# Row maxima and sums of an attention step: spread over the partitions by DMA through DRAM, and merged in the next step

## The chip, the core and the metric

The kernel runs on one core of a Trainium2 chip. The time is the device time of one execution in microseconds (us). The kernel before takes 1843.38 us as the median of three runs (1842.33 to 1845.44).

The engines are PE (TensorE, matrix products), DVE (VectorE), ACT (ScalarE), POOL (GpSimd) and SP (SyncE, which here only issues DMAs). Each works through its own queue of instructions in order. An instruction can wait for semaphores that other engines or DMAs raise; everything behind it on its engine waits too.

## What is computed

A decoder block of 1024 tokens and 1024 channels in float32: an input projection, a state-space branch and an attention branch, their gated sum, then a gated feed-forward network. The change is in the attention branch. There are 3 patterns (dilations 1, 4 and 16) of 8 heads each, with 64 channels a head. The part that matters:

```
s = q @ k.T + bias                       # 128 queries x 256 keys, masked
m = max(s);  p = exp(s - m);  den = sum(p)
o = (p @ v) / den;  lse = m + log(den)   # for each pattern
w = softmax(lse over the 3 patterns)
o_attn = sum(w * o)                      # merged over the patterns
```

The merge needs, for each query, the maximum m and the sum den of each pattern. The kernel keeps a running minimum of -m (`run_n`), a running sum (`run_z`) and a running numerator (`num`) and rescales them as each pattern comes in.

## The kernel before

Products are split in two parts (`whi`, `wlo` for weights, `hhi`, `hlo` for the activations), so that each block of weights takes three products for each piece: hi*hi, hi*lo and lo*hi (L909 to L911). DVE makes `whi` from the loaded `raw` (`hi`, L1673), POOL makes `wlo` (`lo`, L624), and SP loads the next `raw` when `lo` of the block two before is done (L414).

The first 700 us hold 12 attention steps, numbered a = 0 to 11: for each of 4 pairs of heads (hp), the patterns ag = 0, 1, 2. `stage_a` calls `slot` once for each step. A slot runs two things side by side: the projections of q, k and v for the next step n (three blocks b, b+1, b+2), and the attention of step a. It is cut in 12 passes, j = 0 to 11. In each pass PE first computes a quarter of a block (12 products of 512 columns), then what attention needs. Between pattern 1 and 2 there is a block of the state-space branch (`ublock`). The last slot (a = 11) has no next step; it computes instead the last such block and the first block of a gate, and POOL builds there the tables `tb`, `gg` and `gp` of the next stage.

The chain of attention in a slot is this. At even j up to 6, PE computes the scores of two blocks of queries (L1043); DVE adds the mask and takes the row maxima (L1830) and negates them into `negm` (L1834); ACT takes the exponential and its row sums into `den` (L1451); two passes later PE transposes it (L1070), ACT copies it (L1443), and PE multiplies by v (L1057). For the next step, DVE scales each half of a projected block out of PSUM (`evict`, L1796) at odd j; ACT squares it (L1394), PE sums the squares at j = 2, 4, 6, 8 (L923), ACT makes the norm factors `rn`, and POOL multiplies them in (`qk_scale`, L737).

`negm` and `den` have one value for each row, with the queries on the partitions. The merge works with channels on the partitions and queries along the free axis, so each value is needed on 64 partitions. Before, this is done in the same slot: at j = 8 and 9, DVE copies the values into 128 columns each (`stat`, two buffers `hx` and `rtmp`, L1855), and at j = 9, 10 and 11 PE transposes the copies, 16 transposes of 128x128 in a step (L1022, L1031), into PSUM. DVE then merges each half of the queries: `merge_max` (L1755 to L1758), whose result ACT exponentiates into `ab_h` (L1459), `merge_psum` (L1771, L1772) and `merge_z` (L1778, L1780); POOL merges the numerator (`rescale` L765, `weigh` L770, `normalise` L776). The first half is merged at j = 10 and 11 of the slot itself. Of the second half `merge_max` runs at j = 11, the rest in the next slot at j = 0 and 1 (after pattern 1: in `ublock`). For pattern 0 there is nothing to merge with, and the values are only copied.

The order on every engine is that of the code: each engine has its own `slot`, written out by hand, with `if` tests on j.

## Time and profile before

| | |
|---|---|
| median of 3 runs | 1843.38 us |
| the profiled execution: its own time, its span | 1847.69 us, 1845.8 us |
| PE busy | 1795.4 us (97%) |
| DVE busy | 1019.9 us (55%) |
| POOL busy | 828.6 us (45%) |
| ACT busy | 569.2 us (31%) |

The span runs from the first to the last instruction. A busy PE is one with a product in flight: 12 products of 512 columns follow each other at about 0.23 us each, and each is shown with 0.39 us. So the length of a piece of work on PE is read from the chain of work (which has the distance to the next instruction), not from the duration of one product.

The attention slots lie between 57 and 700 us. Slot a = 2 runs from about 168 us, slot a = 3 from about 215 us, the last, a = 11, from about 644 us. The three pairs of heads before the last repeat with the same pattern.

### The profile page before, as it was taken

Reading aid. Unit: us, or ns where it says so; the run is one execution under the profiler, and the core shown is the slowest. Engines: PE = TensorE matmul, PEld = TensorE weight load, DVE = VectorE, ACT = ScalarE, POOL = GpSimd, SP = SyncE. Lnnn points to the kernel's source line nnn. Section 1 sums busy time; section 2 is a strip of 40 time slices with the busy share of each in tenths; the row PEclk is TensorE's granted clock in tenths of the full one; section 3 lists DMA queues with packets and bytes.
Section 4 is the critical chain, followed back from the end, with each engine's and each line's share of the span. In section 5 each row is a group of like instructions: output and inputs, shape, how many; then the busy total and the mean of one; then the engine's idle time right before and its main releaser. Section 6 shows DMA issues by size and latency. Waiting matters only on the chain.

```text
span 1845.8 us, 23996 instructions
## 1 busy us (share of the span) xinstructions
PE 1795.4 (97%) x8628; PEld 1427.0 (77%) x8628; DVE 1019.9 (55%) x1545; ACT 569.2 (31%) x1075; POOL 828.6 (45%) x597
## 2 busy tenths in 40 slices
PE   8999999999999988999899999999999999999997
PEld 6777777777777766788788878788888888888786
DVE  6346645564664587344411232788787787634644
ACT  6533444353344423111411221543333333000000
POOL 7536444653643375554344444265555455222221
PEclk9999999999999998999999999999999999999999
DMA  4111111211111113445411134323223222345211
GB/s 172 35 40 55 47 49 40 76 40 40 47 52 47 40 52 98 110 114 147 139 68 68 68 137 159 137 80 102 69 71 99 68 94 99 126 152 195 85 53 50
DMA packets 64186, 158.00 MB, mean 86 GB/s; under 512 B 10912, under 2 KB 27680, under 8 KB 64112
## 3 DMA queue, kind: packets, MB, share of 16 engines
q1 hardware_dynamic: 51856, 145.35, 23.8%
q10 hardware_dynamic: 11792, 10.04, 2.0%
q0 software_dynamic: 464, 1.62, 0.2%
q8 instruction: 46, 0.75, 0.2%
q14 instruction: 28, 0.23, 0.0%
HBM read 123.54 MB, written 32.26 MB: 84 GB/s over the span
## 4 chain that ended last, share of the span: by engine, by line
PE 73%; issue 12%; DVE 8%; POOL 5%; ACT 1%; DMA 1%; POOLq 0%; SPq 0%; DVEq 0%
PE bank L909 9%; PE bank L911 9%; PE bank L910 9%; PE bank L1278 7%; PE bank L1280 7%; PE bank L1279 7%; PE bank L1336 4%; PE bank L1338 4%; PE bank L1337 4%; PE bank L923 2%; PE bank L1057 2%; PE bank L1070 2%; PE bank L1043 2%; POOL wlo L624 1%; POOL t L858 1%
## 5 line engine op out<-in xcount | busy, mean ns | idle before, releaser
L909 PE MATMUL bank<-hhi,whi 128*128 128x512 f32 x1024 | 421.0, 411 | 5.1 <-DVE hlo L1717 4.6
L911 PE MATMUL bank<-hhi,wlo 128*128 128x512 f32 x1024 | 405.1, 396 | 0.0
L910 PE MATMUL bank<-hlo,whi 128*128 128x512 f32 x1024 | 404.9, 395 | 0.0
L624 POOL TENSOR_TENSOR wlo<-raw,whi 128x1024 fp32r<-128x1024 f32 (+1 forms) x84 | 196.5, 2340 | 281.4 <-DVE whi L1673 279.4
L909 PEld LDWEIGHTS bank<-hhi,whi 128*128 128x128 f32 x1024 | 193.9, 189 | 52.1 <-issue 9.0
L911 PEld LDWEIGHTS bank<-hhi,wlo 128*128 128x128 f32 x1024 | 193.5, 189 | 45.2
L910 PEld LDWEIGHTS bank<-hlo,whi 128*128 128x128 f32 x1024 | 194.2, 190 | 39.6 <-issue 1.2
L1830 DVE CUSTOM_DVE_ANT_0 sp<-bank,mask 128x128 f32<-128x128 f32 (+1 forms) x192 | 56.3, 348 | 113.6 <-PE bank L1043 111.7
L1451 ACT ACTIVATE sp<-sp,negm 128x128 f32<-128x128 f32 (+1 forms) x192 | 83.9, 439 | 107.4 <-DVE negm L1834 107.3
L1673 DVE CAST whi<-raw 128x1024 fp32r<-128x1024 f32 (+1 forms) x84 | 62.3, 741 | 95.1 <-PE bank L911 64.8
L882 POOL TENSOR_TENSOR plo<-st,phi 128x512 fp32r<-128x512 f32 x60 | 79.6, 1329 | 58.7 <-ACT phi L1585 57.4
L2131 DVE CAST fhi<-ff 128x1024 fp32r (+1 forms) x44 | 31.4, 715 | 125.5 <-PE bank L1338 125.5
L1443 ACT ACTIVATE ptr<-bank 128x256 f32<-128x256 f32 (+1 forms) x96 | 45.5, 474 | 165.1 <-PE bank L1070 165.1
L1278 PE MATMUL bank<-thi,phi 128*128 128x512 f32 x240 | 94.8, 395 | 0.0
L1279 PE MATMUL bank<-tlo,phi 128*128 128x512 f32 x240 | 94.7, 395 | 0.0
L1280 PE MATMUL bank<-thi,plo 128*128 128x512 f32 x240 | 94.6, 394 | 0.0
L737 POOL TENSOR_TENSOR kn<-kn,rn 128x512 f32<-128x512 f32 x24 | 35.8, 1493 | 97.9 <-ACT rn L1405 97.9
L882 POOL TENSOR_TENSOR qlo<-pair,qhi 128x512 fp32r<-128x512 f32 x40 | 68.5, 1733 | 13.9 <-ACT qhi L1585 13.9
L1336 PE MATMUL bank<-fhi,whi 128*128 128x512 f32 x176 | 70.2, 399 | 2.3 <-DVE osb L2191 1.4
L895 POOL TENSOR_TENSOR dlo<-raw,dhi 128x1024 fp32r<-128x1024 f32 x11 | 26.8, 2437 | 100.3 <-DVE dhi L2124 100.3
L1338 PE MATMUL bank<-fhi,wlo 128*128 128x512 f32 x176 | 69.5, 395 | 0.0
L1337 PE MATMUL bank<-flo,whi 128*128 128x512 f32 x176 | 69.4, 395 | 0.0
(304 smaller groups left out, 3946.6 us busy)
## 6 DMA issues: line engine op xcount, KB each, us to landing
raw<-in_wblocks SPq DMA_DIRECT2D x98, 512.0 KB, 3.6
pair<-in_wblocks SPq DMA_DIRECT2D x40, 512.0 KB, 4.7
ff_scr<-ffo SPq DMA_DIRECT2D x22, 512.0 KB, 5.9
ff<-ff_scr SPq DMA_DIRECT2D x22, 512.0 KB, 4.0
rt<-rt_scr SPq DMA_DIRECT2D x8, 516.0 KB, 6.8
x<-in_xT SPq DMA_DIRECT2D x8, 512.0 KB, 8.7
zb_scr<-zb SPq DMA_DIRECT2D x8, 512.0 KB, 3.2
zb<-zb_scr SPq DMA_DIRECT2D x8, 512.0 KB, 3.3
```

Of the source, the lines that this page charges most:

```text
L624: pool.tensor_tensor(wlo[par][:, 0:cols], raw[par][:, 0:cols], whi[par][:, 0:cols].bitcast(F32), ALU.subtract).then_inc(lo_done, 1)
L882: pool.tensor_tensor(piece[i][1], weights(u_par)[i], piece[i][0].bitcast(F32), ALU.subtract).then_inc(lo_p, 1)
L909: nc.tensor.matmul(ps, a, x, start=start and k == k_list[0], stop=False)
L910: nc.tensor.matmul(ps, a, y, start=False, stop=False)
L911: last = nc.tensor.matmul(ps, b, x, start=False, stop=stop and k == k_list[-1])
L1278: nc.tensor.matmul(pbank(i), a[:, r], xh, start=c == 0, stop=False)
L1279: nc.tensor.matmul(pbank(i), a[:, r], xl, start=False, stop=False)
L1280: last = nc.tensor.matmul(pbank(i), b[:, r], xh, start=False, stop=c == KC // 2 - 1)
L1336: nc.tensor.matmul(ps, dhi[par][:, r], x, start=start and c == 0, stop=False)
L1337: nc.tensor.matmul(ps, dhi[par][:, r], y, start=False, stop=False)
L1338: last = nc.tensor.matmul(ps, dlo[par][:, r], x, start=False, stop=stop and c == 1)
L1451: last = act.activation(sp[:, s_ % 4, x, s0:], sp[:, s_ % 4, x, s0:], ACT.Exp, bias=negm[:, s_, x:x + 1], accum_out=den[:, s_, x:x + 1])
```

## The change

In the steps a = 0 to 10 the row values go another way. `negm` and `den` are now halves of one tile `sd` of 32 columns. At the end of pass j = 9, PE transposes `sd` once (to 32 partitions of 128), at j = 10 ACT copies the result to `st_t`, and SP writes it to DRAM (`stat_scr`), waits for that, and reads it back four times, each time one row of 1024 values to 64 partitions: into `bmd` (maxima in `bmd[:, 0]`, sums in `bmd[:, 1]`), or for pattern 0 straight into `run_n` and `run_z`. SP does this (`spread`) between its loads of weights. The merge of a step moves as a whole into the next slot: on DVE `merge_max` at j = 1 and 2, `merge_psum` at 3 and 5, `merge_z` at 3 and 6; on ACT the exponential at 3 and 4; on POOL `rescale` and `weigh` at 4 and 6, and `normalise` at 7 and 10 after pattern 2. The product with v at j = 4 and 8 on PE now also waits until `merge_psum` has read the bank. The last step keeps the old way, but its slot now has the whole merge of step 10 in front.

```diff
+            def spread(a, hp, ag):
+                sp_.wait_ge(st_copied, a + 1)
+                sp_.wait_ge(d_read, 2 * a + 1)
+                if ag == 0 and hp:
+                    sp_.wait_ge(o_ready, 2 * hp)
...
+                sp_.dma_start(stat_scr.rearrange("i x (s q) -> (i x s) q", q=P), st_t[0:32, :]).then_inc(st_out, 16)
+                sp_.wait_ge(st_out, 16 * (a + 1))
+                for i, done in enumerate((sm_in, sz_in)):
+                    to = (run_n, run_z)[i][:, :] if ag == 0 else bmd[:, i, :]
+                    for x in range(2):
+                        sp_.dma_start(to[DH * x:DH * (x + 1)], stat_scr[i, x].unsqueeze(0).broadcast_to([DH, T])).then_inc(done, 16)
...
 # POOL, slot
-                    if a and ag == 0 and j == 0:
-                        weigh(a - 1, 2, hp - 1, 1)
-                    if a and ag == 0 and j == 5:
-                        normalise(2, hp - 1, 1)
+                    if a and ag != 1 and j in (4, 6):
+                        pg, ph, h = (ag + 2) % 3, hp - (ag == 0), j // 2 - 2
+                        rescale(pg, ph, h)
+                        weigh(a - 1, pg, ph, h)
+                    if a and ag == 0 and j in (7, 10):
+                        normalise(2, hp - 1, j == 10)
...
 # PE, slot
-                    if a is not None and j in (9, 11):
+                    if n is None and j in (9, 11):
...
+                                if a and s_ % 4 == 0:
+                                    pe.wait_ge(d_read, 2 * a + s_ // 4)
...
+                        if n is not None and j == 9:
+                            pe.wait_ge(ln_done, 4 * n + 4)
+                            nc.tensor.transpose(b_nb[0:32, 0:P], sd[:].rearrange("p i x s -> p (i x s)"), ident).then_inc(mt_done, 1)
...
 # ACT, slot
+                    if a and ag != 1 and j in (3, 4):
+                        weights_exp((ag + 2) % 3, hp - (ag == 0), j - 3)
...
+                        act.activation(st_t[0:32, :], b_nb[0:32, 0:P], ACT.Copy).then_inc(st_copied, 1)
...
 # DVE, merge_max and slot
-                nn, ps = natural(run_n[:, :], ag, h), split2(b_nb[:], ag)
+                if a == LAST:
+                    dve.wait_ge(mt_done, LAST + h + 1)
+                else:
+                    dve.wait_ge(sm_in, 32 * (a + 1))
+                nn, new = natural(run_n[:, :], ag, h), split2(b_nb[:] if a == LAST else half(bmd[:, 0, :], h), ag)
...
-                TT(t_z[:], b_t[:], ab[h][:, 1, :], ALU.mult).then_inc(d_read, 1)
+                TT(t_z[:], b_t[:] if a == LAST else half(bmd[:, 1, :], h), ab[h][:, 1, :], ALU.mult).then_inc(d_read, 1)
...
+                    if a:
+                        last_step = a - 1, (ag + 2) % 3, hp - (ag == 0)
+                        if j in (1, 2):
+                            merge_max(*last_step, j - 1)
+                        if j in (3, 5):
+                            merge_psum(*last_step, j == 5)
+                        if j in (3, 6):
+                            merge_z(*last_step, j == 6)
...
-                    if a is not None and j in (8, 9):
+                    if n is None and j in (8, 9):
```

Two places show how the order moves. The first is DVE in slot a = 3, from the end of pass 0 to the first score of pass 2. Before:

```order
L1834 TENSOR_SCALAR negm<-mx 128x4 [waits dve_c]
L1771 TENSOR_TENSOR t_num<-bank,ab_h 128x512 [waits ab_exp,dt_done,pv_done]
L1772 TENSOR_TENSOR t_z<-bank,ab_h 128x512
L1796 TENSOR_TENSOR qn<-bank,rs 128x128x4 [waits groups]
L1820 COPY vv<-bank 128x512 [waits vt_done]
L1673 CAST whi<-raw 128x1024 [waits groups,loaded0]
L1778 TENSOR_TENSOR run_z<-run_z,ab_h 128x8x64
L1780 TENSOR_TENSOR run_z<-run_z,t_z 128x8x64 [waits d_read,dve_c]
L1830 ISA sp,mx<-bank,mask 128x256 [waits dve_c,s_done,h_lo]
```

After these come the other scores of pass 2, their `negm`, and then at once the second eviction of q (L1796). Now, from the last instruction of the scores of pass 2 to the cast of pass 4 (L1886 was L1834, L1846 was L1796, L1723 was L1673):

```order
L1886 TENSOR_SCALAR sd<-mx 128x2x2 [waits dve_c]
L1802 TENSOR_TENSOR ab_h<-run_n,bmd 128x512 [waits merged,sm_in]
L1803 TENSOR_TENSOR run_n<-run_n,bmd 128x8x64 [waits dve_c]
L1806 TENSOR_SCALAR ab_h<-ab_h 128x512 [waits dve_c]
L1807 TENSOR_SCALAR ab_h<-ab_h 128x512 [waits dve_c]
L1846 TENSOR_TENSOR qn<-bank,rs 128x128x4 [waits groups]
L1821 TENSOR_TENSOR t_num<-bank,ab_h 128x512 [waits ab_exp,sz_in,pv_done]
L1822 TENSOR_TENSOR t_z<-bmd,ab_h 128x512
L1828 TENSOR_TENSOR run_z<-run_z,ab_h 128x8x64
L1830 TENSOR_TENSOR run_z<-run_z,t_z 128x8x64 [waits d_read,dve_c]
L1723 CAST whi<-raw 128x1024 [waits dve_c,groups,loaded1]
```

The same four instructions of `merge_max` for the first half stand between the cast of pass 1 and the scores of pass 2. So the second eviction has eight more instructions ahead of it in this slot, and two of `merge_z` fewer.

The second place is POOL in the last slot. Before, the second merge of the numerator (L765, L770) of step 10 stands ahead of the tables:

```order
L765 TENSOR_TENSOR num<-num,ab_h 128x2x256 [waits ab_exp]
L770 TENSOR_TENSOR num<-num,t_num 128x2x256 [waits d_read,pool_c]
L624 TENSOR_TENSOR wlo<-raw,whi 128x1024 [waits hi_done]
L711 TENSOR_TENSOR tb<-ccr,b_in 128x1024 [waits bc_in,prep_b]
L712 TENSOR_TENSOR ttmp<-cci,b_in 128x8x128 [waits pool_c]
L713 TENSOR_TENSOR tb<-tb,ttmp 128x1024 [waits pool_c]
L624 TENSOR_TENSOR wlo<-raw,whi 128x1024 [waits pool_c,hi_done]
L721 TENSOR_TENSOR gg<-g_a,c_in 128x1152
```

Now (L804 was L765, L809 was L770, L661 was L624, L748 to L750 were L711 to L713, L758 to L760 were L721 to L723):

```order
L750 TENSOR_TENSOR tb<-tb,ttmp 128x1024 [waits pool_c]
L804 TENSOR_TENSOR num<-num,ab_h 128x2x256 [waits pool_c,ab_exp]
L809 TENSOR_TENSOR num<-num,t_num 128x2x256 [waits d_read,pool_c]
L661 TENSOR_TENSOR wlo<-raw,whi 128x1024 [waits hi_done]
L758 TENSOR_TENSOR gg<-g_a,c_in 128x1152
L759 TENSOR_TENSOR ttmp<-g_b,c_in 128x1152 [waits pool_c]
L760 TENSOR_TENSOR gg<-gg,ttmp 128x1152 [waits pool_c]
L758 TENSOR_TENSOR gp<-g_c,c_in 128x1024 [waits pool_c]
L759 TENSOR_TENSOR ttmp<-g_d,c_in 128x8x128 [waits pool_c]
L760 TENSOR_TENSOR gp<-gp,ttmp 128x1024 [waits pool_c]
L804 TENSOR_TENSOR num<-num,ab_h 128x2x256 [waits pool_c,ab_exp]
L809 TENSOR_TENSOR num<-num,t_num 128x2x256 [waits d_read,pool_c]
```

The first half of the numerator is merged between `tb` and `gg`, the second after all six instructions of `gg` and `gp`.

## Rows read from the trace of the kernel before

**Rows 1.** The page: busy time, share of the span, instructions.
```profile
PE 1795.4 (97%) x8628; PEld 1427.0 (77%) x8628; DVE 1019.9 (55%) x1545; ACT 569.2 (31%) x1075; POOL 828.6 (45%) x597
```

**Rows 2.** Windows, slots 3 and 11: length; busy PE, PEld, DVE, ACT, POOL; clock; DMA, GB/s.
```profile
213.00:255.00 42.00, 40.32 (x219) 30.04 (x218) 27.29 (x60) 25.69 (x55) 23.55 (x13) 1.00 0.12 38
...
663.00:700.00 37.00, 32.44 (x175) 24.72 (x174) 31.23 (x35) 16.11 (x33) 26.96 (x13) 0.95 0.19 65
```

**Rows 3.** Chain of work, step 0: start, length on the chain, what.
```profile
98.08 0.44 PE bank L1022 x4
```

**Rows 4.** Timeline of DVE, slot 3: start, length, instruction, [idle before <- releaser].
```profile
225.09 0.67 DVE L1673 CAST whi<-raw 128x1024 fp32r<-128x1024 f32 x1
...
226.74 3.09 DVE L1780 TENSOR_TENSOR run_z<-run_z,t_z 128x512 f32<-128x512 f32 x1
...
231.65 1.05 DVE L1834 TENSOR_SCALAR negm<-mx 128x4 f32<-128x4 f32 x1
232.60 1.10 DVE L1796 TENSOR_TENSOR qn<-bank,rs 128x512 f32<-128x512 f32 x1
```

**Rows 5.** Timeline of POOL, slot 3.
```profile
225.84 3.05 POOL L624 TENSOR_TENSOR wlo<-raw,whi 128x1024 fp32r<-128x1024 f32 x1 [0.77 <-DVE whi L1673]
...
231.13 1.53 POOL L737 TENSOR_TENSOR qn<-qn,rn 128x512 f32<-128x512 f32 x1
```

**Rows 6.** Timelines of DVE and POOL at the end of slot 1.
```profile
157.96 2.41 POOL L624 TENSOR_TENSOR wlo<-raw,whi 128x1024 fp32r<-128x1024 f32 x1 [0.71 <-DVE whi L1673]
158.90 1.09 DVE L1756 TENSOR_TENSOR run_n<-run_n,bank 128x512 f32<-128x512 f32 x1
```

**Rows 7.** Timeline of DVE, end of slot 2: one half of the merge.
```profile
215.18 1.04 DVE L1755 TENSOR_TENSOR ab_h<-run_n,bank 128x512 f32<-128x512 f32 x1
...
217.69 0.43 DVE L1758 TENSOR_SCALAR ab_h<-ab_h 128x512 f32<-128x512 f32 x1
```

**Rows 8.** Timelines of PE and ACT, slot 3.
```profile
222.30 0.60 PE L1005 MATMUL bank<-cst_s,vt 128*128 128x128 f32 x4
...
234.72 1.08 ACT L1394 ACTIVATE sq<-qn 128x512 f32<-128x512 f32 x1
235.95 1.10 PE L923 MATMUL bank<-sq,cst_s 128*128 128x512 f32 x2 [1.38 <-ACT sq L1394]
```

**Rows 9.** Timelines of DVE, ACT and PE, slot 2.
```profile
176.33 1.03 DVE L1673 CAST whi<-raw 128x1024 fp32r<-128x1024 f32 x1
...
184.20 0.62 ACT L1394 ACTIVATE sq<-qn 128x512 f32<-128x512 f32 x1
185.82 1.02 PE L923 MATMUL bank<-sq,cst_s 128*128 128x512 f32 x2
```

**Rows 10.** Timelines of DVE and POOL, last slot.
```profile
653.15 0.68 DVE L1820 COPY vv<-bank 128x512 f32<-128x512 f32 x1
...
663.28 2.05 DVE L1673 CAST whi<-raw 128x1024 fp32r<-128x1024 f32 x1
...
685.95 1.03 DVE L1755 TENSOR_TENSOR ab_h<-run_n,bank 128x512 f32<-128x512 f32 x1
...
657.67 2.66 POOL L711 TENSOR_TENSOR tb<-ccr,b_in 128x1024 f32<-128x1024 f32 x1
...
679.25 2.47 POOL L723 TENSOR_TENSOR gp<-gp,ttmp 128x1024 f32<-128x1024 f32 x1
```

**Rows 11.** Chain of work, last slot: start, length on the chain, what.
```profile
664.39 0.43 PE bank L909
...
667.17 0.23 PE bank L910
...
711.23 0.70 DVE zb L1789
```

**Rows 12.** DMA issues, 57 to 700 us: count, KB each, median us to landing.
```profile
raw<-in_wblocks SPq DMA_DIRECT2D x36, 512.0 KB, 3.5
...
u_scr<-utmp SPq DMA_DIRECT2D x4, 512.0 KB, 2.6
```

More of the change, by code:

```diff
@@ L189, in bass_hybrid_block @@
             mx = sb("mx", [P, 2, 2])
-            negm = sb("negm", [P, 8, 2])
-            den = sb("den", [P, 8, 2])
+            sd = sb("sd", [P, 2, 2, 8])
+            st_t = sb("st_t", [P, P])
             utmp = sb("utmp", [P, CH, NCH])
-            rtmp = sb("rtmp", [P, 2, GB, NCH // 2])
-            hx = sb("hx", [P, T])
+            bmd = sb("bmd", [P, 2, T])
             with ExitStack() as s_prep:
@@ L285, in bass_hybrid_block @@
         dhi, dlo = (dhi0, whi[1]), (dlo0, wlo[1])
-        stat = [hx[:], rtmp[:].rearrange("p a g k -> p (a g k)")]
+        negm, den = sd[:, 0], sd[:, 1]
+        stat = [bmd[:, h, :] for h in range(2)]
+        LAST = 3 * HP - 1
         bank = [ctx.enter_context(nc.psum_tensor(f"bank{i}", [P, HT], F32)) for i in range(8)]
@@ L453, in _ @@
                                   [:, bass.ds(RSTEP * hp, RB)], rt0[NST * u:NST * (u + 1)]).then_inc(rt_out, 16)
-            for n in range(B_AEND, B_E1 + 1):
+            for n in range(B_AEND, B_AEND + 3):
                 load(n, wblocks[n], n % 2)
+            spread(LAST - 3, HP - 2, 2)
+            for n in range(B_AEND + 3, B_AEND + 6):
+                load(n, wblocks[n], n % 2)
+            spread(LAST - 2, HP - 1, 0)
+            for n in range(B_AEND + 6, B_E1 + 1):
+                load(n, wblocks[n], n % 2)
+            spread(LAST - 1, HP - 1, 1)
             sp_.wait_ge(pv_done, 8 * 11)
@@ L1023, in slot @@
                         last.then_inc(mt_done, 1)
-                    if a is not None and j in (10, 11):
+                    if n is None and j in (10, 11):
                         h = j - 10
@@ L1451, in slot @@
                                 last = act.activation(sp[:, s_ % 4, x, s0:], sp[:, s_ % 4, x, s0:], ACT.Exp,
-                                                      bias=negm[:, s_, x:x + 1], accum_out=den[:, s_, x:x + 1])
+                                                      bias=negm[:, x, s_:s_ + 1], accum_out=den[:, x, s_:s_ + 1])
                             last.then_inc(exp_done, 1)
@@ L1833, in slot @@
                         link(last)
-                        V.tensor_scalar(negm[:, j:j + 2, :], mx[:], -1.0, None, ALU.mult).then_inc(smx_done, 1)
-                    if a and (ag < 2 or n is None) and j == 0:
-                        merge_psum(a - 1, (ag + 2) % 3, hp - (ag == 0), 1)
-                    if a is not None and j == 11:
+                        V.tensor_scalar(negm[:, :, j:j + 2].rearrange("p x s -> p s x"), mx[:], -1.0, None, ALU.mult).then_inc(smx_done, 1)
+                    if n is None and j == 11:
                         merge_psum(a, ag, hp, 0)
@@ L1861, in slot @@
                         gate_in(0, 0, j - 10)
-                    if a is not None and j >= 10:
+                    if n is None and j >= 10:
                         merge_max(a, ag, hp, j - 10)
-                    if a is not None and j == 11:
+                    if n is None and j == 11:
                         merge_z(a, ag, hp, 0)
-                        if n is None:
-                            merge_psum(a, ag, hp, 1)
-                            merge_z(a, ag, hp, 1)
+                        merge_psum(a, ag, hp, 1)
+                        merge_z(a, ag, hp, 1)
                 if n is None:
```

102 lines of the change are left out of this document (57 added, 45 removed).

## The prediction

> **What bounds the kernel now.** I read the page first: PE is busy for 97% of the span [rows 1]. Work taken off PE in the attention part is worth its full length, as long as nothing makes PE wait instead. So the question is what PE waits for in the slots, and whether the change adds to it. The windows of the slots show PE busy all the time but for two kinds of place: slot 3 (and 6 and 9, which repeat it) has 40.32 us of work in 42.00, and the last slot 32.44 in 37.00 at a mean clock of 0.95 [rows 2]. The timelines say why. In slot 3, PE stands for 1.38 us before the second sum of squares, until ACT has squared the second half of q; ACT stands behind the eviction of q by DVE, which DVE only reaches at 232.60 [rows 8, 4]. In slot 2 the same instruction starts without idle time, since the square ended at 184.82, a microsecond ahead [rows 9]. In the last slot the chain runs through DVE and ends at the gate's eviction at 711.23 [rows 11]: there DVE, not PE, sets the time.
>
> A second thing decides this case: DVE and POOL get in each other's way. In slot 3 the last addition to `run_z` takes 3.09 us, while `lo` is on POOL from 225.84 to 228.89 [rows 4, 5]; it ends 0.94 us after POOL's instruction does, so it stood until then. The negation of 4 values takes 1.05 us, until the end of POOL's multiplication [rows 4, 5]. But the minimum with a source in PSUM takes its usual 1.09 us in the middle of a `lo` of normal length [rows 6]. So an instruction of DVE with all its operands in SBUF waits for the instruction that POOL has begun, and one that reads PSUM does not.
>
> The Trainium skill (SBUF — State Buffer, on the shared port pair) states the same and more: a DVE instruction with two SBUF inputs and a GpSimd instruction that reads SBUF exclude each other for a whole instruction, whoever starts first. It speaks against this change, which moves a source of three DVE instructions of each half of the merge from PSUM to SBUF. By this rule, the trace agrees (3.09 against 1.09 us). Without it the sum below would come out faster; that case is a rival.
>
> **What goes.** Per step, 16 transposes in four groups, each of them 0.44 us on the chain of work [rows 3], 1.76 us; one transpose comes, at a quarter of a group, 0.11 us, or 0.2 if it costs a change of weights. I take 1.6 us a step. There are 11 such steps: -17.6 us. It counts fully, since in passes 9 to 11 PE does not wait. The copies of `negm` and `den` and the copies for pattern 0 leave DVE too, at passes where DVE has spare time; I count them at nothing.
>
> **What the new way costs by itself.** ACT's copy, SP's store and four loads are new waits: `merge_max` in pass 1 waits for the maxima. The trace has no such transfer. Lower bound: the store as `u_scr`, 2.6 us, the loads as one load of 512 KB, 3.5 us, so 6.1 us; upper bound: five such transfers one behind the other, 2.6 + 4 x 3.5 = 16.6 us [rows 12]. Four passes lie between, 10, 11, 0 and 1, of 12 products at 0.23 us and some 1 us of attention each, together 15 us. The loads are issued without waiting for each other, so I take 8 us, hidden. Loads of weights queued behind them on SP have two blocks, some 25 us, in hand. I count 0 for this, and +1 us a merge, 7 in all, at the far end.
>
> **Slots 3, 6 and 9 (merge of pattern 2).** DVE in pass 1: the eviction can start when the products end at 222.30 [rows 8]; with the copy of v and the cast (0.97 + 0.6 + 0.6 us from start to start) `merge_max` begins at 224.5. Uncontended a half takes 2.9 us, from 215.18 to 218.12 [rows 7]. But the cast has just released POOL's `lo` of 2.4 us, and it shares operands in SBUF only: the subtraction goes first, `lo` follows, the minimum waits for it. That makes 1.1 + 2.4 + 1.1 + 0.9 = 5.4 us, to 229.9. Scores of pass 2 then take 1.5 us, the negation 1.05 as before [rows 4]: 232.5. The second half: 2.9 us, to 235.4; eviction 1.0, to 236.4; square 1.1 [rows 8], to 237.5. PE arrives at 235.95 - 1.38 = 234.6. It waits 3.0 us instead of 1.4: +1.6. Behind this the lock takes its toll once more: DVE's last pair (L1778, L1780) and the negation of pass 6 alternate with `rescale`, `weigh` and `qk_scale`, so that the fourth square is about 1 us late for PE in pass 8. I take +2.5 us a slot. The ends: without the lock, the square is ready 2.4 us sooner and PE waits 0.6 us, -0.8; with one more wait for a `lo`, +3.2.
>
> **Slots 2, 5 and 8 (merge of pattern 1).** Same sequence, shorter passes of 128 columns. The cast starts at 176.33 [rows 9]; `merge_max` begins at 176.9, ends 5.4 us later at 182.3 (2.9 us if the lock didn't bind: 179.8), scores 1.1, negation 0.6 (POOL multiplies q), second half 2.9, eviction 0.6, square 0.6 [rows 9]: 188.1. PE comes at 185.82 [rows 9]. It waits 2.3 us where it did not wait. The ends are 0 (without the lock, 185.7 is in time) and +3.2. I take +2.3.
>
> In slots 1, 4, 7 and 10 the merge is only a copy of the numerator, so nothing is late: 0.
>
> **The last slot.** Here DVE is the bound. Before, `merge_max` of step 10 was done by 647.5, beside products. Now DVE is idle until its copy of v (653.15 before [rows 10], some 1.2 us earlier now) and then has 2.9 + 2.9 + 1.3 + 2.2 = 9.3 us of merge ahead of the cast of the gate's second block, where it had 4.9. The cast, at 663.28 before [rows 10], comes 3.2 us later uncontended. But POOL has `lo` and three instructions of `tb` (2.66 us the first [rows 10]) in the same stretch; each can hold an instruction of DVE for about 2 us, together up to +6. The cast frees POOL for the tables, which ended at 681.7 [rows 10]; behind them now stand `rescale` and `weigh` of the second half (1.6 us each), and DVE's second `merge_max` of step 11 (685.95 before [rows 10]) needs them. With the cast 3.2 us late: 681.7 + 3.2 + 3.2 = 688.1, +2 us. With 9 us, and 2 more for DVE's merge among the tables: 681.7 + 11 + 3.2 = 695.9, +10. There is no row for this alternation at length; I take +9, near the upper end, since [rows 4, 10] show nearly every such meeting at its full price. What follows up to 711.23 is serial and moves with it [rows 11].
>
> **Sum.** -17.6 + 3 x 2.5 + 3 x 2.3 + 9 = +5.8 us. Against the profiled execution, 1847.7 + 5.8 = 1853.5 us. That execution lies 4.3 us over the median of the runs, so the forecast is 1843.4 + 5.8, about 1849 us. The bounds of the terms: -17.6 - 2.4 + 0 + 2 = -18.0, and -17.6 + 9.6 + 9.6 + 10 = +11.6, with transfers that come late +18.6.
>
> The clock can add to this. In the last slot, after waits, six products are 0.43 us apart instead of 0.23 [rows 11], so the engine ran at 1.2 instead of 2.4 GHz for that stretch: 1.2 us lost. The wait of 1.38 us in slot 3 was followed by no such stretch (clock 1.00 [rows 2]). Waits of 2 to 3 us are in between; if each of the six did it, +7 us.
>
> **Rivals.**
> 1. *PE keeps nearly all it is given: faster.* The lock binds little and the queue on DVE has the slack to take the merge. For it: DVE is busy for only 55% [rows 1], its idle time lies just in these passes, and 4 us of copies leave it in each step. Against it: the minimum of `merge_max` meets `lo` by construction, since the cast ahead of it starts `lo`. With slots at -0.8 and 0 and the last at +5: -15 us, 1828.
> 2. *A draw.* Terms of about half the size: slots at +1 and +1.2, last slot +7: -4 us, 1840, or a little less gain, 1843.
> 3. *The transfers come late.* If the chain store, wait, four loads takes the 16.6 us of the upper bound and SP's queue adds to it, DVE stands in pass 1 with evictions behind it. Every microsecond beyond the 15 counts in six slots. At 3 us late, on top of the forecast: +18, 1867. Against it: the queue of SP is free at that point, having nothing but loads that wait for `lo`.
> 4. *The slots lose more than they gain, worse than forecast:* the clock falls in the waits. +7 us, 1856.
>
> **Chances.** Forecast with its neighbourhood (1847 to 1854) 0.33; rival 1 0.27; rival 2 0.2; rival 4 0.14; rival 3 0.06. The likeliest alone has 1845 to 1856. The range goes from 1827 to 1859: it takes in the bounds of the terms and leaves out the far transfers. A difference of 0.2% (3.7 us) is what can be told from no change. Faster by more: rival 1 and a third of rival 2, 0.34. Within: the rest of rival 2 and the edge of the forecast, 0.18. Slower by more: 0.48.
>
> **What would show it.** The transposes: on PE one instruction of 32 columns a step and a slot shorter by 1.6 us where no merge is (slots 1, 4, 7 and 10). The lock: the minimum of the first half at over 3 us instead of 1.1, in the middle of a `lo`. The queue: PE's idle time before the second sum of squares, 3.0 us in slot 3 and 2.3 in slot 2, released by ACT's square. The last slot: the cast of the second gate block some 8 us later from the slot's start, `merge_max` of the second half behind POOL's `weigh`. The transfers: DVE not waiting for DMA in pass 1. The forecast is wrong if ACT's squares come in time, that is, if slots 2 and 3 show PE at 38 of 38 and 42 of 42 us; or if DVE's wait in pass 1 names a DMA.

## The result and the profile after

The changed kernel takes 1862.2 us (median of 4 runs, 1859.2 to 1863.6); the kernel before took 1844.4 us beside it (4 runs, 1842.3 to 1845.8). The ratio is 1.0097, with a 95% interval of 1.0084 to 1.011: 17.9 us slower. The forecast was about 1849 us, by its sum 5.8 us slower, and its range ended at 1859. The profiled execution took 1861.9 us, its span 1860.0.

The table takes each slot from the start of its first transpose of v to that of the next slot, and the last slot from there to the gate's eviction [rows 11].

| slots | before, us | after, us | change of all |
|---|---|---|---|
| 0, 1, 4, 7, 10 (nothing to weigh) | 52.4, 61.1, 61.1, 61.1, 50.0 | 50.8, 59.5, 59.5, 59.5, 48.4 | -8.0 |
| 2, 5, 8 (merge of pattern 1) | 47.2, 47.2, 47.2 | 50.1, 50.1, 50.1 | +8.8 |
| 3, 6, 9 (merge of pattern 2) | 54.1, 54.2, 54.2 | 55.5, 56.6, 55.5 | +5.1 |
| last | 64.2 | 76.9 | +12.7 |

Together that is +18.6 us. What follows the last slot took 1134.6 us in the profile before and 1130.4 after. In the experiments that stretch lay anywhere from 1128.6 to 1134.6, whatever the edit, so I take nothing from this difference.

The page's busy line (busy time, share of the span, instructions) answers to [rows 1]:

```profile
PE 1787.9 (96%) x8463; PEld 1411.8 (76%) x8463; DVE 999.4 (54%) x1485; ACT 570.1 (31%) x1086; POOL 822.0 (44%) x597
```

PE has 165 instructions and 7.5 us of work fewer, not 17.6: some of its instructions got longer. The windows of slot 2, slot 3 and the last slot (length; busy PE, PEld, DVE, ACT, POOL; granted clock; DMA, GB/s) answer to [rows 2]:

```profile
175.00:213.00 38.00, 35.45 (x182) 25.62 (x181) 24.87 (x48) 17.60 (x48) 18.51 (x11) 0.96 0.15 49
213.00:255.00 42.00, 38.68 (x203) 28.05 (x202) 29.50 (x61) 22.35 (x51) 16.54 (x9) 0.96 0.19 51
663.00:700.00 37.00, 21.98 (x113) 16.09 (x112) 36.24 (x52) 9.29 (x33) 27.37 (x13) 0.72 0.20 64
```

The clock, at 1.00 before in slot 3, is at 0.96, and in the last slot at 0.72 where it was 0.95. DVE is now busy for all but 0.8 of 37 us there. PE's timelines in slots 2 and 3 (start, length, instruction, [idle before <- releaser]) answer to [rows 8, 9]:

```profile
185.01 1.10 PE L961 MATMUL bank<-sq,cst_s 128*128 128x512 f32 x2 [2.46 <-ACT sq L1434]
186.04 1.23 PE L1080 MATMUL bank<-kn,qn 64*128 64x128 f32 x8
187.20 1.12 PE L1096 MATMUL bank<-ptr,vv 128*64 128x128 f32 x8
...
236.84 1.69 PE L961 MATMUL bank<-sq,cst_s 128*128 128x512 f32 x2 [3.32 <-ACT sq L1434]
```

The waits stand where the forecast put them, at 2.46 us (forecast 2.3) and 3.32 us (3.0). Behind the first, eight score products take 1.23 us and eight products with v 1.12. Where no such wait stands, both take about 0.7 (a row of such a run follows below): PE worked at 1.2 instead of 2.4 GHz there. Such a time at the lower clock is a slow stretch in what follows. DVE and POOL in slot 2, which answer to [rows 6, 7]:

```profile
173.66 3.08 POOL L661 TENSOR_TENSOR wlo<-raw,whi 128x1024 fp32r<-128x1024 f32 x1 [3.99 <-DVE whi L1723]
...
174.61 3.06 DVE L1803 TENSOR_TENSOR run_n<-run_n,bmd 128x512 f32<-128x512 f32 x1
...
181.58 1.10 DVE L1803 TENSOR_TENSOR run_n<-run_n,bmd 128x512 f32<-128x512 f32 x1
...
183.52 0.68 DVE L1846 TENSOR_TENSOR qn<-bank,rs 128x512 f32<-128x512 f32 x1
```

The minimum of the first half meets `lo` and takes 3.06 us; that of the second half takes 1.10. In slot 3 it is 3.08. The eviction stands behind both halves. In the last slot, DVE's first `merge_max`, PE's three long waits, DVE's copies of the row values, the `weigh` that POOL does behind the tables, and the gate's eviction answer to [rows 10, 11]:

```profile
658.00 1.31 DVE L1802 TENSOR_TENSOR ab_h<-run_n,bmd 128x512 f32<-128x512 f32 x1
659.34 2.65 DVE L1803 TENSOR_TENSOR run_n<-run_n,bmd 128x512 f32<-128x512 f32 x1
662.03 1.93 DVE L1806 TENSOR_SCALAR ab_h<-ab_h 128x512 f32<-128x512 f32 x1
663.99 2.45 DVE L1807 TENSOR_SCALAR ab_h<-ab_h 128x512 f32<-128x512 f32 x1
...
667.54 1.22 PE L1080 MATMUL bank<-kn,qn 64*128 64x128 f32 x8 [3.36 <-DVE sd L1886]
...
672.74 1.12 PE L1096 MATMUL bank<-ptr,vv 128*64 128x128 f32 x8 [3.98 <-issue]
...
687.73 9.29 DVE L1911 COPY bmd<-sd 128x512 f32<-128x512 f32 x4
...
692.48 1.11 PE L1059 MATMUL bank<-cst_s,bmd 128*128 128x128 f32 x4 [5.84 <-DVE bmd L1911]
...
698.66 1.57 POOL L809 TENSOR_TENSOR num<-num,t_num 128x512 f32<-128x512 f32 x1
...
729.57 0.69 DVE L1839 TENSOR_TENSOR zb<-bank,rs 128x512 f32<-128x512 f32 x1
```

Every one of the four instructions of `merge_max` meets one of POOL's, and it takes 8.4 us instead of 2.9. The copies of the row values start 35.1 us from the slot's start, where they started 25.0 us from it before, and the four take 9.3 us instead of 7.4. The transfers, from 57 to 700 us, answer to [rows 12] (count, KB each, median us to landing):

```profile
bmd<-stat_scr SPq DMA_DIRECT2D x28, 256.0 KB, 4.5
...
stat_scr<-st_t SPq DMA_DIRECT2D x11, 16.0 KB, 1.4
```

In no slot does DVE wait for them.

### The profile page after: what moved, and what is told of

Read it like the earlier page. It is cut to its first block, busy times and chain, and to the rows that moved or that the text cites. A ratio compares the mean times of both kernels' runs of the same rounds, so it can differ in the third digit from the quotient of the medians.

```text
span 1860.0 us, 23700 instructions
## 1 busy us (share of the span) xinstructions
PE 1787.9 (96%) x8463; PEld 1411.8 (76%) x8463; DVE 999.4 (54%) x1485; ACT 570.1 (31%) x1086; POOL 822.0 (44%) x597
## 4 chain that ended last, share of the span: by engine, by line
PE 72%; issue 12%; DVE 10%; POOL 5%; DMA 1%; ACT 1%; POOLq 0%; SPq 0%; DVEq 0%
PE bank L947 9%; PE bank L949 9%; PE bank L948 9%; PE bank L1318 7%; PE bank L1320 7%; PE bank L1319 7%; PE bank L1376 4%; PE bank L1378 4%; PE bank L1377 4%; PE bank L961 2%; PE bank L1096 2%; PE bank L1080 2%; PE bank L1107 2%; DVE run_n L1803 2%; POOL wlo L661 1%
## 5 line engine op out<-in xcount | busy, mean ns | idle before, releaser
L661 POOL TENSOR_TENSOR wlo<-raw,whi 128x1024 fp32r<-128x1024 f32 (+1 forms) x84 | 197.4, 2350 | 401.9 <-DVE whi L1723 400.4
L1498 ACT ACTIVATE sp<-sp,sd 128x128 f32<-128x128 f32 (+1 forms) x192 | 83.9, 439 | 185.4 <-DVE sd L1886 185.4
L1723 DVE CAST whi<-raw 128x1024 fp32r<-128x1024 f32 (+1 forms) x84 | 64.3, 765 | 96.5 <-PE bank L949 63.5
L1846 DVE TENSOR_TENSOR vt<-bank,rs 128x512 f32<-128x512 f32 x24 | 23.3, 969 | 141.3 <-PE bank L949 141.3
L933 POOL TENSOR_TENSOR dlo<-raw,dhi 128x1024 fp32r<-128x1024 f32 x11 | 26.8, 2436 | 99.5 <-DVE dhi L2179 99.5
L961 PE MATMUL bank<-sq,cst_s 128*128 128x512 f32 x96 | 53.2, 637 | 17.6 <-ACT sq L1434 17.3
```

What stands on the lines that cost most here:

```text
L661: pool.tensor_tensor(wlo[par][:, 0:cols], raw[par][:, 0:cols], whi[par][:, 0:cols].bitcast(F32), ALU.subtract).then_inc(lo_done, 1)
L961: nc.tensor.matmul(b_nb[:], blk_ones, sq[:, gi % 2, :], start=True, stop=True).then_inc(ss_done, 1)
L1498: last = act.activation(sp[:, s_ % 4, x, s0:], sp[:, s_ % 4, x, s0:], ACT.Exp, bias=negm[:, x, s_:s_ + 1], accum_out=den[:, x, s_:s_ + 1])
```

## The experiments

Each kernel ran five rounds beside the kernel before; the figures are differences from it, by the ratio of the runs, with the interval. Most intervals are some 2.5 us to either side. The changed kernel stands at +17.9. Unless said otherwise an edit is made to the changed kernel.

**1. The second eviction ahead of the second half.**

```
-                        if j in (1, 2):
-                            merge_max(*last_step, j - 1)
+                        if j in (1, 2 if n is None else 3):
+                            merge_max(*last_step, j > 1)
```

> The changed kernel, but in the slots with projections the second half of merge_max stands in DVE's pass 3, behind the second eviction of q, instead of ahead of it. Queue theory: ACT's second square comes 2.9 us sooner, the wait of PE before the second sum of squares (3.3 us in slot 3, 2.5 in slot 2) falls to under 0.5 us in each of the six slots, and with it the stretch at the lower clock behind it (granted clock 1.00 again in slots 2 and 3): 6 x (2.5 to 3 of wait + 1.2 to 1.5 of slow products) less what the half merge now delays behind it, -14 to -22 us, 1840 to 1848 us. Lock rival: the delay is made by POOL's lo in the first half, which stays where it is, so at most 1 us a slot comes back: 1856 or more. Route rival: the DMA chain sets the time, nothing changes: 1862. The last slot, which keeps its order, stays at 12 to 13 us over before in each case.

Measured: +7.9 us (1.0043, 1.003 to 1.0057), 10 us less than the change. Slots 2 and 3 take 48.6 and 54.5 us. PE and ACT in slot 2, and PE in slot 3:

```profile
182.03 1.04 ACT L1478 ACTIVATE ab_h<-ab_h 128x1024 f32<-128x1024 f32 x1
182.98 0.61 ACT L1434 ACTIVATE sq<-qn 128x512 f32<-128x512 f32 x1
...
183.73 1.10 PE L961 MATMUL bank<-sq,cst_s 128*128 128x512 f32 x2 [1.32 <-ACT sq L1434]
184.76 0.71 PE L1080 MATMUL bank<-kn,qn 64*128 64x128 f32 x8
...
234.13 1.84 PE L961 MATMUL bank<-sq,cst_s 128*128 128x512 f32 x2 [2.28 <-ACT sq L1434]
```

The order of the queue matters, but less than expected: only 1.1 us of the wait went in slot 2 and 1.0 in slot 3, since ACT, held up by the late negation, now comes to the square after the exponential of the weights. The slow stretch went too in slots 2, 5 and 8, where the wait is 1.32 us (clock 1.00). Where it is 2.28 us, slots 3 and 6 have one (0.96 in slot 3's window) and slot 9 has none (1.00), yet all three take 54.4 to 54.5 us: at the full clock, PE waits 1.1 us more for the fourth square. So a slow stretch can cost nothing where another chain is close.

**2. The cast behind the first half.**

```
+                        if n is not None and j == 1:      # behind merge_max
+                            hi(b + 1, (par0 + 1) % 2, need=2 * b)
```

> The changed kernel, but in pass 1 the cast of the next weights, which releases POOL's lo, stands behind the first half of merge_max instead of ahead of it. Lock theory: the minimum takes 1.1 us instead of 3.06, the second square comes about 2 us sooner, PE's wait falls from 3.3 to about 1.3 us in slot 3 and from 2.5 to about 0.5 in slot 2; the clock falls in fewer slots: 6 x 2 to 3.5, -12 to -20 us, 1842 to 1850. Its price: the cast comes 4 us later, and the weights of the next block with it, which has passes in hand. Queue theory alone (the order of the eviction decides, not the meeting with lo): POOL's lo then meets the negation or the second half, and the 2 us are paid there: -3 to +2, 1859 to 1864. Route rival: no change.

Measured: +12.5 us (1.0068, 1.0054 to 1.0082), 5.4 less than the change; between the two theories. DVE in slot 2:

```profile
174.30 1.08 DVE L1803 TENSOR_TENSOR run_n<-run_n,bmd 128x512 f32<-128x512 f32 x1
...
177.87 1.55 DVE L1886 TENSOR_SCALAR sd<-mx 128x4 f32<-128x4 f32 x1
...
180.44 2.04 DVE L1803 TENSOR_TENSOR run_n<-run_n,bmd 128x512 f32<-128x512 f32 x1
...
183.32 0.68 DVE L1846 TENSOR_TENSOR qn<-bank,rs 128x512 f32<-128x512 f32 x1
```

With `lo` out of its way the first minimum takes 1.08 us. That is the lock shown by taking away what it meets: the two instructions are the same as before. But the 2 us are mostly paid again at the negation (1.55) and the second minimum (2.04, beside POOL's multiplication of q), and the eviction comes only 0.5 us sooner, 15.6 us from the slot's start instead of 16.1. So PE's wait in slot 2 is 1.96 us instead of 2.46, and the clock still falls behind it (0.96 from 171 to 213 us):

```profile
184.81 1.69 PE L961 MATMUL bank<-sq,cst_s 128*128 128x512 f32 x2 [1.96 <-ACT sq L1434]
```

The Trainium skill (SBUF — State Buffer, section Terms, on the shared port pair) says that the loser of the pair is blocked for the whole instruction of the other, and that it does not share bandwidth. The trace agrees (3.06 us beside `lo`, 1.08 us without it).

**3. Tables of the last slot behind the merge.**

```
                     if n is None and j == 4:
                         lo(B_E1 + 1, 1)
+                    if n is None and j == 6:      # POOL, behind rescale and weigh
                         g_table(0)
                         gp_table(0)
```

> The changed kernel, but in the last slot POOL does the two gate tables (six instructions, some 15 us) behind rescale and weigh of the second half of step 10 instead of ahead of them. Theory of POOL's order: DVE's second merge_max of step 11 (704.0 in the changed kernel) no longer stands behind weigh at 698.7, and the last slot gets 4 to 8 us shorter, 1854 to 1858 us; the tables end 3 us later, which PE needs only behind the gate. Rival, the lock with the tb table: the 8.4 us of the first merge_max in that slot and the late cast at 678 are made before this point, and the tables then collide with the stat copies and the gate: gain 0 to 2 us, 1860 to 1862.

Measured: +16.0 us (1.0087, 1.0072 to 1.0102); the last slot takes 76.6 us against 76.9. The rival was right. POOL's `weigh` now comes 15.4 us sooner from the slot's start, and the second `merge_max` of step 11 only 0.2 us:

```profile
680.63 2.29 POOL L809 TENSOR_TENSOR num<-num,t_num 128x512 f32<-128x512 f32 x1
...
701.22 1.04 DVE L1803 TENSOR_TENSOR ab_h<-run_n,bank 128x512 f32<-128x512 f32 x1
```

In the changed kernel `weigh` had ended at 700.23, 3.8 us before that `merge_max` began at 704.01. So it was never what DVE waited for there.

**4. The thinned transposes alone (kernel before).**

```
-                        for s_ in range(4):
+                        for s_ in range(1 if n is not None else 4):
                             last = nc.tensor.transpose(b_nb[:, s_ * P:(s_ + 1) * P], ...
```

> The kernel before, with one part of the change alone: of the four transposes of each group of negm and den only the first is done in the slots with projections (88 + 88 of 176 transposes in 11 steps become 44 instead of 176), while the merge stays where it was; so maxima and sums are wrong in three quarters of the rows, and one Ln is an Exp. Theory (PE's time counts in full): 12 transposes of about 0.11 us a step, 11 steps: -14.5 us, 1829 us. Rival (the waits of slots 3, 6 and 9 and the clock take part of it): -8 to -10 us, 1834 to 1836. Were it under -4, the gain of the change would be off the path altogether.

This kernel leaves out transposes that the result needs, and one Ln, so its values are wrong; it serves for the time alone. Measured: -7.8 us (0.9958, 0.9944 to 0.9972). That is near the rival (-8 to -10). By slots: 1, 4 and 7 are 1.2 to 1.3 us shorter, 3, 6 and 9 0.7 to 0.8, and 2, 5 and 8 only 0.2 to 0.3. In slot 2 PE stood for POOL:

```profile
182.76 0.50 PE L909 MATMUL bank<-hhi,whi 128*128 128x512 f32 x1 [0.68 <-POOL wlo L624]
```

PE was busy for the whole of slot 2 before, and still a microsecond taken off it there bought next to nothing, as the weights were not split yet.

**5. Also the square ahead of the weights on ACT** (on top of 1).

```
...
+                    if a and ag != 1 and n is not None and j == 3:    # ACT, behind square
+                        weights_exp((ag + 2) % 3, hp - (ag == 0), 0)
```

> As the run with the second eviction ahead of the second half of merge_max (1852.4 us), and on ACT the exponential of the first half's weights (1.04 us) stands behind the square in pass 3 instead of ahead of it. There the wait before the second sum of squares had fallen from 3.3 to 2.3 us in slot 3 and from 2.5 to 1.3 us in slot 2, and ACT's row showed exponentials of the scores, then the weights (1.04 us), then the square, without idle time. Theory (the rest of the wait is ACT's queue behind a late negation): each of the six waits gets 1.04 us shorter, to 1.3 and 0.3 us, and slots 2 and 3 with it: -6 us or, with less time at the low clock, -9: 1843 to 1847. Rival (the time is lost in the passes behind, the third and fourth squares): -2 us or less, 1850 to 1853.

Measured: +7.4 us (1.004, 1.0026 to 1.0054), as without this edit: the theory fell, the rival holds. PE's rows with idle time:

```profile
182.98 1.10 PE L961 MATMUL bank<-sq,cst_s 128*128 128x512 f32 x2 [0.38 <-ACT sq L1434]
185.59 0.66 PE L1096 MATMUL bank<-ptr,vv 128*64 128x128 f32 x8 [0.87 <-issue]
...
233.35 1.10 PE L961 MATMUL bank<-sq,cst_s 128*128 128x512 f32 x2 [1.34 <-ACT sq L1434]
...
244.35 1.10 PE L961 MATMUL bank<-sq,cst_s 128*128 128x512 f32 x2 [1.19 <-ACT sq L1434]
```

The first wait did get 0.94 us shorter in both slots, and new ones took its place: 0.87 us ahead of the products with v in slot 2, 1.19 at the third square in slot 3. The clock is 1.00 in both slots now, and slot 3 takes 54.8 us, no less than with the slow stretch of run 1 (54.5).

**6. Both halves behind the eviction** (on top of 5).

```
+                        if n is not None and j == 3:
+                            merge_max(*last_step, 0)
+                            merge_max(*last_step, 1)
```

> As the run before this one, and the first half of merge_max too stands behind the second eviction, so DVE does in pass 1 to 3: copy, cast, scores, negation, eviction, and then both halves of the merge. Theory (one queue: merge ahead of the scores delays negation, exponentials, square): the second square comes as in the kernel before or sooner; PE's wait there is under 0.8 us in each slot and the clock of slots 2 and 3 is 1.00. The lock moves too, since lo now meets the negation. Slots 2 and 3 reach 46.9 and 53.4 us, their lengths in the run with thinned transposes: 1840 us, with the last slot still 12 us over. Rival: the merge of 8.6 us now stands ahead of merge_psum, which PE's product with v needs in pass 4, or delays the third eviction, and the wait appears there: 1845 to 1852.

Measured: +20.7 us (1.0112, 1.0096 to 1.0127), slower than the change. Neither theory gave that size. The place is the rival's. DVE and PE in slot 2:

```profile
186.73 0.68 DVE L1823 TENSOR_TENSOR t_num<-bank,ab_h 128x512 f32<-128x512 f32 x1
187.33 0.68 DVE L1824 TENSOR_TENSOR t_z<-bmd,ab_h 128x512 f32<-128x512 f32 x1
...
188.11 0.66 PE L1096 MATMUL bank<-ptr,vv 128*64 128x128 f32 x8 [3.77 <-issue]
```

The numerator of the step before still lies in the PSUM bank into which pass 4 writes the first products with v. So the merge has only the first passes of the slot: early, it holds up the eviction; late, it holds up PE. This is the bind of the change, and my forecast did not have it, although the change itself names the new wait.

**7. Step 10 merged the old way.** The 16 transposes and the copies of step 10 are back, its merge stands in its own passes 10 and 11, and the last slot is that of before.

```
+        OLD = (LAST - 1, LAST)
...
-                    if n is None and j in (9, 11):
+                    if a in OLD and j in (9, 11):
```

> The changed kernel, but step 10 too is merged the old way (16 transposes in its own slot, the merge in its passes 10 and 11 and in passes 0 and 1 of the last slot), so that the last slot is that of the kernel before. Theory (the last slot as such costs 12.7 us, by the merge that moved into it): that comes back less 1.6 us of transposes in slot 10: -11 us, 1851. Rival (the last slot is late for reasons that remain, such as the stat copies that meet POOL's tables): -3 to -5 us, 1857 to 1859.

Measured: +6.5 us (1.0035, 1.0023 to 1.0047), 11.4 less than the change, as expected. The gate's eviction, 76.9 us from the start of the last slot in the change, comes at 718.69, 65.1 from it:

```profile
718.69 0.69 DVE L1846 TENSOR_TENSOR zb<-bank,rs 128x512 f32<-128x512 f32 x1
```

This run shows one thing more. Slot 2 has the instructions of the changed kernel and the same wait, 2.46 us, but no slow stretch behind it. PE there, and the window of slot 2:

```profile
184.82 1.10 PE L962 MATMUL bank<-sq,cst_s 128*128 128x512 f32 x2 [2.46 <-ACT sq L1441]
185.84 0.71 PE L1085 MATMUL bank<-kn,qn 64*128 64x128 f32 x8
```

```profile
175.00:213.00 38.00, 35.45 (x189) 25.79 (x188) 24.61 (x48) 17.70 (x48) 19.30 (x11) 1.00 0.21 64
```

The slot takes 48.6 us where it takes 50.1 in the changed kernel, at 0.96. With the same instructions and the same wait, the difference of 1.5 us is the price of the slow stretch.

**8. A longer route.**

```
+                for k in range(4):      # the store four times, each waited for
...
```

> The changed kernel with the store of the statistics done four times, each waited for before the next (3 more round trips of 1.4 us by the profile of the change, some 4.5 us in all), ahead of the four loads. Theory (the route is hidden: in the changed kernel the loads land 8 us or more ahead of merge_max): no change, 1862 within 2 us, and no wait of DVE on a DMA. Rival (route on the path): 4.5 us in each of six slots, 1885 or more.

Measured: +17.9 us (1.0097, 1.0081 to 1.0112), no change. The loads of slot 1 are issued 7.1 us after the first store instead of 1.4, and DVE still waits for none. The route through DRAM is hidden.

**9. The new route for pattern 0 alone (kernel before).** Steps of pattern 0, whose merge is a copy, take the new route; the others keep transposes and place.

```
-                    if a is not None and j in (9, 11):
+                    if ag and j in (9, 11):            # the old transposes
...
+                        if ag == 0 and j == 9:         # the new one
```

> The kernel before, with the new route (one transpose, ACT's copy, store, four loads) for the steps of pattern 0 alone, whose merge is a mere copy; steps of patterns 1 and 2 keep their 16 transposes and their merge in passes 10 and 11. So no merge_max moves, and 4 of 11 steps lose their transposes. Theory (the gain of PE is real where PE is the bound, the loss comes from the merge that moved): slot 0 gives 1.6 us, slots 3, 6 and 9 some 0.9 each (there the thinned run gave 0.7 of 1.3), the last slot stays: -4.3 us, 1841 us, the first version that beats before. Rival (moved waits eat it, or the route disturbs): 1844 to 1847.

Measured: -7.2 us (0.9961, 0.9948 to 0.9974): faster than before, by more than expected. Slots 3, 6 and 9 give 1.6 to 1.7 us each instead of 0.9. DVE's copies, which are gone there too, may be the reason; no run takes them apart.

**10. Edits 1, 2 and 7 together.**

```
+                        if j in (1, 3):
+                            merge_max(*last_step, j > 1)
...
+                    if a and n is not None and j == 1:
+                        hi(b + 1, (par0 + 1) % 2, need=2 * b)
```

> The changed kernel with three repairs that worked by themselves, put together: second half of merge_max behind the second eviction (-9.8 us alone), cast behind the first half of merge_max (-4.7 alone), and step 10 merged the old way (-9.4 alone). Theory (three separate places): the last adds fully, of the first two half of the second remains: 1862 - 9.8 - 2.4 - 9.4 = 1840.6 us, faster than before by 4. Rival (the slots are bound by the loop through ACT and DVE, so that each repair gives its place to the next wait, as in the two runs with the square and both halves moved): slots 2 and 3 stay at 48.5 and 54.5, 1843 to 1846, no gain on before.

Measured: -7.2 us (0.9961, 0.9948 to 0.9974), the theory, and 3 us better. It is 25.1 us less than the change; the three alone sum to 26.8. Windows of slots 2 and 3, and PE there:

```profile
167.00:215.00 48.00, 46.40 (x243) 34.12 (x242) 29.54 (x63) 20.00 (x57) 22.46 (x14) 1.00 0.30 85
215.00:258.00 43.00, 40.55 (x227) 29.50 (x226) 30.34 (x61) 26.70 (x58) 21.52 (x12) 1.00 0.12 37
```

```profile
184.56 0.66 PE L1101 MATMUL bank<-ptr,vv 128*64 128x128 f32 x8 [0.58 <-issue]
...
231.59 1.10 PE L962 MATMUL bank<-sq,cst_s 128*128 128x512 f32 x2 [0.51 <-ACT sq L1441]
```

All waits are under 1.1 us and the clock is 1.00 in both slots. Both faster kernels, this one and number 9, get to the same time. (Number 4 is faster too, but does not compute the result.)

**11 and 12. A wait made to measure (kernel before).** Three memsets, or five, ahead of the second eviction. My expectations name slots 2, 5 and 8; the edit takes the steps of pattern 1, which stand in slots 1, 4, 7 and 10. So there are four waits, not three.

```
+                    if ag == 1 and j == 3:
+                        for _ in range(3):             # 5 in the second run
+                            link(V.memset(hx[:], 0.0))
```

> The kernel before, with three memsets of 0.9 us on DVE ahead of the second eviction in slots 2, 5 and 8: the second square comes 2.5 us later, 1.5 us behind PE, which had 1 us of slack there. Clock theory (a wait of 1.3 us leaves the granted clock at 1.00, one of 2.3 us does not): the three slots get some 1.5 us longer, clock 1.00 in them: +4.5 us, 1849.5. Rival (any wait lowers the clock): +8 us or more. Rival (later waits are absorbed): +1 or less.

> The same with five memsets: the square is 3.4 us behind PE in slots 2, 5 and 8. Clock theory: each wait of 3.4 us is followed by a stretch at 1.2 GHz that costs another 1.2 to 1.5 us, so these slots get 4.6 to 4.9 us longer and show a granted clock below 0.97: +14 to +15 us, 1859. Without a cost of the clock: 3 x 3.4 = +10 us, 1855.

Measured: +5.3 us (1.0029, 1.0018 to 1.0039) and +22.9 us (1.0124, 1.0107 to 1.0141). PE in slot 1 with three memsets:

```profile
126.58 1.09 PE L923 MATMUL bank<-sq,cst_s 128*128 128x512 f32 x2 [1.08 <-ACT sq L1394]
127.61 0.93 PE L1043 MATMUL bank<-kn,qn 64*128 64x128 f32 x8
```

and with five:

```profile
128.62 1.10 PE L923 MATMUL bank<-sq,cst_s 128*128 128x512 f32 x2 [3.39 <-ACT sq L1394]
129.65 1.64 PE L1043 MATMUL bank<-kn,qn 64*128 64x128 f32 x8
131.22 1.60 PE L1057 MATMUL bank<-ptr,vv 128*64 128x128 f32 x12
```

A wait of 1.08 us makes slot 1 1.3 us longer, at a clock of 1.00. One of 3.39 us makes it 5.1 us longer: the products behind it take 1.64 instead of 0.93, and the clock from 120 to 140 us is 0.91. Four such slots give 5.1 and 20.7 us. The clock's share is at most 5.1 - 3.4 = 1.7 us a wait, since the short wait, too, made its slot 0.2 us longer than itself.

**13 and 14. The last slot taken apart.** First, the `tb` table on POOL in pass 4 instead of pass 0; then, separately, both halves of `merge_max` behind the scores of pass 2.

```
-                        pool.wait_ge(prep_b, 2)
-                        tb_table(0)
                     if n is None and j == 4:
+                        pool.wait_ge(prep_b, 2)
+                        tb_table(0)
```

```
-                        if j in (1, 2):
-                            merge_max(*last_step, j - 1)
+                        if j == 2 and n is None:
+                            merge_max(*last_step, 0)
+                            merge_max(*last_step, 1)
```

> The changed kernel, but in the last slot POOL does the tb table (three instructions, 7.5 us) in pass 4, behind rescale and weigh of the first half of step 10, instead of in pass 0. Lock theory: the first merge_max there (8.4 us from 658.0) keeps only its meeting with lo and takes 4.5 to 5.5 us; the scores of pass 2 and all behind them come 3 us sooner, and so does the end of the tables: -3 us or more, 1859 or less. Rival (what costs is that the merge stands ahead of the scores at all, or POOL's total of 37 us of work in that slot, wherever it lies): 0 to -1 us, 1861 to 1862.

> The changed kernel, but in the last slot both halves of merge_max stand behind the scores of pass 2 instead of around them. If the merge ahead of the scores is what costs there, PE's wait of 3.4 us for the negation goes and the last slot gets 3 us shorter or more: 1859 or less. Rival (as with both halves moved in the other slots, PE's product with v in pass 4 then waits for merge_psum): the wait of 4.0 us before that product grows by what the other lost: 1862 or more.

Measured: +15.1 us (1.0082, 1.0068 to 1.0096) and +17.3 us (1.0094, 1.008 to 1.0108). In the first the minimum is alone:

```profile
660.55 1.08 DVE L1803 TENSOR_TENSOR run_n<-run_n,bmd 128x512 f32<-128x512 f32 x1
...
668.89 0.66 PE L1096 MATMUL bank<-ptr,vv 128*64 128x128 f32 x8 [2.85 <-issue]
```

`merge_max` takes 3.3 us instead of 8.4, and the last slot 75.0 instead of 76.9: of 5.1 us at its start 1.9 arrive at its end. POOL works without a pause from 671 to 700 there, and DVE meets it elsewhere: the last two instructions of the first `merge_max` of step 11 take 1.41 and 1.65 us instead of 0.63 and 0.43. In the second run the last slot takes 77.8 us: PE's wait for the negation is gone, and the one ahead of the products with v grew from 3.98 to 8.91 us:

```profile
670.90 1.12 PE L1096 MATMUL bank<-ptr,vv 128*64 128x128 f32 x8 [8.91 <-issue]
```

## Why the prediction was wrong

The direction was right, and most of the mechanism. The step that failed is the clock, which the sum put at nothing. Two more sizes failed to the same side.

- **Transposes, -1.6 us a step.** Right in the five slots without a merge (-8.0 us; forecast -8.0). The sentence that they count fully in the others, since PE does not wait in passes 9 to 11, failed. With thinned transposes, worth 1.3 us where PE is the bound, slots 2, 5 and 8 gave 0.2 to 0.3 us and slots 3, 6 and 9 some 0.8. A busy PE does not say that its work is worth its length; another loop was within a microsecond of it, in slot 2 that of the cast and `lo`.
- **The lock.** Right: 3.06 and 3.08 us for the first minimum, 1.08 once the cast was moved. So was the point that the meetings come again: taking one away moved most of the 2 us to the next.
- **PE's waits.** 2.46 and 3.32 us where 2.3 and 3.0 were forecast; right. The further microsecond at the fourth square did not show.
- **The clock.** This is the step that failed. "Waits of 2 to 3 us are in between; if each of the six did it, +7 us" was a rival with a chance of 0.14, and I had left it out of the sum on the strength of one wait of 1.38 us that was followed by no slow stretch. In the changed kernel all six did it: 0.96 in slots 2 and 3, down to 0.92 in slot 6 (378 to 420 us). The price can be read from equal slots. Six kernels here (the changed one and runs 3, 7, 8, 13 and 14) have the same order in slots 2, 5 and 8 and the same wait of 2.45 to 2.47 us. Of these 18 slots three have no slow stretch and take 48.6 us; 14 have one and take 50.0 to 50.1; one has a longer one (0.93) and takes 51.1. So it costs 1.4 us, once 2.5, and it does not come every time. In slots 3, 6 and 9 of the same kernels, with waits of 3.3 us, it came in all 18: 13 take 55.4 to 55.5 us and five, at a clock of 0.94, take 56.6 to 56.9. Slot 6 of the changed kernel is one of the five; in other runs it is another slot, so nothing in slot 6 itself makes it so. What a slow stretch costs in these slots is only a difference: in slot 3 the wait grew by 1.9 us and the transposes took up to 1.6 off, while the slot grew by 1.3, so up to 1.0 us is the clock's.
- **Slots 2, 5 and 8:** forecast +0.7 us each, measured +2.9. The clock is 1.5 of it. At a clock of 1.00 (slot 2 of run 7) the slot is still 1.4 us longer than before: PE waits 2.5 us, and its busy time falls by 1.1 instead of 1.6. **Slots 3, 6 and 9:** forecast +0.9, measured +1.3 to +2.5. The clock made up for a term of mine that did not show, the further microsecond at the fourth square; that the forecast for slots 3 and 9 is so near is in part luck.
- **Last slot, +9.** Measured 12.7. The 8.4 us of `merge_max` and the late cast (9.2 us later from the slot's start; "some 8") were right. The path through `weigh` was wrong: it does not set the time (run 3). DVE's own queue does, which is busy for 36.2 of 37 us: 10.1 us of the delay are there when the copies of the row values begin, and 1.9 more when they end. What each of its meetings with POOL would cost alone stays open. Repairs in one place brought 0.3 and 1.9 us, or cost 0.9; not moving the merge brings nearly all.
- **Transfers.** Right to count them at nothing; 5.7 us more were hidden as well.

What the forecast did not have at all is the bank of the numerator: the merge must end before pass 4 writes there. It cost nothing in the changed kernel's slots with projections, but it stops the obvious repair (run 6).

In the sum, 6.7 us of the miss lie in slots 2, 5 and 8 (4.4 of them by the clock), 2.4 in slots 3, 6 and 9, and 3.7 in the last slot. (A slip of 0.1 us, 1.1 + 2.4 + 1.1 + 0.9 taken as 5.4, changes none of this.)

## What to carry to other kernels

Before work is taken off the busiest engine, look how late the next chain is: where it is within a microsecond, the gain ends there and becomes a wait. Price a new wait on PE by its length while it is a microsecond or so. Once it comes near two, put a slow stretch behind it into the sum, with its chance: here it cost 1.4 us, most times but not each time, and nothing where another chain was close. When work is moved to a later stage, look up which buffer it holds and who writes there next; apply the move first where the work is only a copy, which here kept the gain (-7 us) without the loss.

## What the hardware showed unexpectedly

The price of a wait is not its length: 1.08 us cost 1.3 us, 3.39 us cost 5.1, on the same instruction of the same kernel. Nor does the length alone decide. Inside the slots with projections, no wait up to 1.5 us has a slow stretch behind it, each of 3.3 us and more has one, and so have the six of 1.96 and 2.68 us of run 2. But the wait of 2.46 us has one in 15 of 18 equal slots, and that of 2.28 us in two of three. What decides in between, the runs do not say.

A small transfer through DRAM to all partitions was cheap: the store of 16 KB took 1.4 us and each load of 256 KB 4.5, with the four issued together.
